# How two streamed weight panels inside the state-space scan reach TensorE: plain float32, or split in high and low parts

## The reference, cut to what matters

```
(z_s, xbc, dt_s, qkv, z_d, b_d, a_d, gate_s, gate_d) = split(u @ w_in[l])
y_s = ssd_chunked(xs, dt, a, Bm, Cm) + xs * d_skip            # the scan, two chunks of 128 tokens
yg  = y_s * silu(z_s);  yg = yg * rsqrt(mean(yg*yg per group)) * norm_w
merged = sigmoid(gate_s) * (y_s @ ssm_w_branch) + sigmoid(gate_d) * (y_d @ dn_w_branch)
h = h + merged @ w_out
```

## Time and profile before

| what | value |
|---|---|
| median of three executions | 2237.24 us |
| the profiled execution's own time | 2238.61 us |
| its span, first to last instruction | 2236.7 us |
| TensorE matmul busy | 2130.2 us (95%) |
| VectorE busy | 1332.4 us (60%) |
| ScalarE busy | 1136.3 us (51%) |
| GpSimd busy | 81.5 us (4%) |
| mean granted TensorE clock | 0.985 of full |
| plain matmul records, line 600 | 384 |

### The profile page before, as it was taken

The page is one execution under the profiler, slowest core; times in us unless marked ns, Lnnn a source line. Parts: engine busy times, 40 slices in busy tenths (PEclk is TensorE's granted clock), DMA queues, the critical chain, the costliest instruction groups (busy, mean ns, idle before and its releaser), DMA issues. The chain is left out here.

```text
span 2236.7 us, 40879 instructions
## 1 busy us (share of the span) xinstructions
PE 2130.2 (95%) x15572; PEld 1863.2 (83%) x15572; DVE 1332.4 (60%) x1845; ACT 1136.3 (51%) x1673; POOL 81.5 (4%) x90
## 2 busy tenths in 40 slices
PE   5999889999999999989999999999999998999998
PEld 4787778887888988888998887887997897998887
DVE  3436375556556986566656555555896575756554
ACT  3453644445445556654445445445556664535444
POOL 0000000000000011100000000000002010000000
PEclk9999999999999999989999999999999999999999
DMA  9663245554553544421455554555444431455553
GB/s 395 240 243 114 76 144 186 188 188 173 186 189 137 179 169 132 170 96 58 151 188 184 188 188 169 184 187 186 145 176 146 156 114 41 141 181 187 188 188 122
DMA packets 53319, 373.08 MB, mean 167 GB/s; under 512 B 6305, under 2 KB 6305, under 8 KB 9281
## 3 DMA queue, kind: packets, MB, share of 16 engines
q1 hardware_dynamic: 47664, 342.00, 42.4%
q0 software_dynamic: 5520, 29.23, 3.7%
HBM read 370.10 MB, written 1.11 MB: 166 GB/s over the span
## 5 line engine op out<-in xcount | busy, mean ns | idle before, releaser
L1443 ACT ACTIVATE HI<-ring 128x1024 fp32r<-128x1024 f32 x606 | 625.1, 1054 | 741.2 <-PE banks L548 399.3
L1987 DVE TENSOR_TENSOR LO<-ring,HI 128x1024 fp32r<-128x1024 f32 x318 | 389.1, 1226 | 368.8 <-ACT HI L1443 368.4
L1993 DVE TENSOR_TENSOR LO<-ring,HI 128x2048 fp32r<-128x2048 f32 x137 | 314.3, 2294 | 242.3 <-ACT HI L1443 242.3
L512 PE MATMUL banks<-UH,HI 128*128 128x256 f32 x1392 | 406.5, 292 | 2.7 <-DVE LO L1993 2.7
L513 PE MATMUL banks<-UL,HI 128*128 128x256 f32 x1392 | 395.9, 284 | 0.0
L514 PE MATMUL banks<-UH,LO 128*128 128x256 f32 x1392 | 395.6, 284 | 0.0
L546 PE MATMUL banks<-HI,UH 128*128 128x512 f32 x896 | 350.0, 391 | 7.1 <-DVE LO L1993 4.9
L547 PE MATMUL banks<-LO,UH 128*128 128x512 f32 x896 | 349.4, 390 | 0.0
L548 PE MATMUL banks<-HI,UL 128*128 128x512 f32 x896 | 349.4, 390 | 0.0
L512 PEld LDWEIGHTS banks<-UH,HI 128*128 128x128 f32 x1392 | 268.8, 193 | 19.8 <-issue 19.1
L513 PEld LDWEIGHTS banks<-UL,HI 128*128 128x128 f32 x1392 | 269.2, 193 | 1.4 <-issue 1.2
(11 more groups left out here) (329 smaller groups left out, 3092.7 us busy)
## 6 DMA issues: line engine op xcount, KB each, us to landing
ring<-in_w_stream SPq DMA_DIRECT2D x315, 1024.0 KB, 4.8
ARENA<-in_ada_stream POOLq DMA_DIRECT2D x16, 1024.0 KB, 5.5
ARENA<-in_ada_stream SPq DMA_DIRECT2D x8, 1024.0 KB, 14.8
GRMS<-cum_rows POOLq DMA_DIRECT2D x16, 256.0 KB, 3.6
ARENA<-in_na_bias POOLq DMA_DIRECT2D x2, 1024.0 KB, 13.4
RMS<-cum_rows POOLq DMA_DIRECT2D x8, 256.0 KB, 3.4
RSTD<-cum_rows POOLq DMA_DIRECT2D x8, 256.0 KB, 3.5
ARENA<-in_ropes POOLq DMA_DIRECT2D x1, 1088.0 KB, 19.1
```

What stands on the lines that cost most here:

```text
L512: nc.tensor.matmul(out, lh, rh, start=start, stop=False, **kw)
L1443: nc.scalar.activation(HI[:, q % PARTS, at], ring[:, q % RING, at], ACT.Copy).then_inc(hi_ready, 1)
L1987: nc.vector.tensor_tensor(LO[:, q % PARTS, at], ring[:, q % RING, at], HI[:, q % PARTS, at].bitcast(F32), ALU.subtract).then_inc(lo_ready, 1)
L1993: nc.vector.tensor_tensor(LO[:, q % PARTS, :], ring[:, q % RING, :], HI[:, q % PARTS, :].bitcast(F32), ALU.subtract).then_inc(lo_ready, 2)
```

## The change

The range of plain panels is cut to 20 to 23, and a new constant `EARLY` = 26 takes over where the code meant the first panel after the scan. Panels 24 and 25 are used in split form within the scan. Three things in the code change and one follows without a changed line:

- TensorE calls `wide_half` instead of `plain_half` in steps 12 to 15.
- GpSimd gets two calls of `split`, for panels 24 and 25, behind its last `load_rows` and ahead of the adding of squares.
- The loop after the scan and VectorE's early low part go by `EARLY`, so panel 26 is treated as before.
- In ScalarE's code the test `if j + PARTS not in PLAIN: ahead(LQ_WIDE + j)` now holds for j = 22 and 23. So in its steps 11 and 13 it writes `HI` of panel 24 and 25, ahead of the `conv_in` of those steps, and `conv_in` no longer counts on `hi_ready` for them. The counters that show panels 24 and 25 as finished become the ordinary ones.

```
-PLAIN = range(20, 26)
+PLAIN = range(20, 24)
+EARLY = 26
...
                     load_rows(i)
+                for j in range(PLAIN[-1] + 1, EARLY):
+                    split(Q_LAYERS + LQ_WIDE + j, L_PANELS * l)
...
                     if i in Z_SLOTS:
                         j, e = Z_SLOTS[i]
-                        plain_half(w0 + j, Q_LAYERS + LQ_WIDE + j, rounds, j % 2, e)
+                        wide_half(w0 + j, Q_LAYERS + LQ_WIDE + j, rounds, j % 2, e)
...
-                    if L_CONV + j not in PLAIN:
+                    if L_CONV + j >= EARLY:
                         for e in range(2):
                             wide_half(w0 + L_CONV + j, Q_LAYERS + LQ_WIDE + L_CONV + j, rounds, j % 2, e,
-                                      l + 1 if L_CONV + j == PLAIN[-1] + 1 else None)
+                                      l + 1 if L_CONV + j == EARLY else None)
...
-                q26 = Q_LAYERS + LQ_WIDE + PLAIN[-1] + 1
+                q26 = Q_LAYERS + LQ_WIDE + EARLY
```

## The result

The changed kernel takes 2245.95 us (median of nine executions, 2241.13 to 2246.9); the kernel before, on the same chip, takes 2237.5 (nine, 2234.84 to 2239.43). The ratio is 1.0037, its 95% interval 1.0028 to 1.0045: 8.5 us or 0.37% slower. The profiled execution took 2246.9 us, its span is 8.4 us longer than that of before.

The account below looks back on a forecast made before the run. TensorE's own instructions were taken to bound scan steps 12 to 15. Stall 4.0 + clock 1.4 - matmuls 1.75 = 3.65 us a layer, 7.3 in two, gave a median of 2244.5 us, range 2240.3 to 2249.5.

Parts of the forecast that it names:

- Bound: Scan steps 12 to 15: TensorE's own instructions set the time, busy all 18.0 us, with a beat of 4.73 us.
- Matmuls: TensorE's halves in steps 12 to 14 each get 0.58 us shorter; three count, 1.75 us a layer.
- High parts: ScalarE's 1.99 us a panel before `conv_in` in steps 11 and 13 costs nothing, hidden with 0.6 us to spare.
- Low parts: GpSimd's subtraction for panel 24 waits for panel 23's last matmul; TensorE stands still 4.0 us, ends 3.76 and 5.1.
- 0.5 us is left: VectorE's `scan_out(7)` behind panel 26's subtraction, 902.5, against release by TensorE at about 903: 0.5 us of slack.
- Rival E: VectorE, shut out twice by GpSimd, brings `scan_out(14)`, `scan_out(15)` or panel 26 late: 2 us more a layer, 2250; chance 0.06.
- Clock: TensorE runs at half clock behind the idle stretch before panel 24: 1.4 us a layer, between 0 and 2.9.
- the sum: Per layer 4.0 (stall) + 1.4 (clock) - 1.75 (matmuls) = 3.65 us; two layers 7.3.
- Rival A: The forecast: one stall before panel 24 in each layer and half clock behind it, 2241.7 to 2249.6 us; chance 0.70.
- B: The stall before panel 24 without a fall of the clock: 2.3 us a layer, 2241.7 (2240.4 to 2244); chance 0.13.
- D: The stall happens, but a later wait, on squares or VectorE, takes most back: 2238 to 2239 us; chance 0.06.
- C: Panel 24's `LO` is there in time, the matmuls' gain stands alone: 3.5 to 4.5 us less, 2233.3; chance 0.05.

Follow-up runs that it names:

- early subtraction: The changed kernel, with GpSimd subtracting for panel 24 once its high part is there, on its own semaphore, not waiting for panel 23: 2236.71 us, ratio 0.9992.
- the filled stall: The changed kernel, with 33 unneeded matmuls on TensorE ahead of its wait for panel 24's low part: 2243.31 us, ratio 1.0023.
- the second measurement: The changed kernel measured again without an edit, on the chip of the experiments: 2244.84 us against 2238.31 before the change, ratio 1.0030.
- the swap: VectorE's last `scan_out` put ahead of panel 26's subtraction; here in the changed kernel with 33 unneeded matmuls before TensorE's wait: 2244.01 us, ratio 1.0027.
- the four kernels with an early low part: The changed kernel with GpSimd early; that with VectorE's last `scan_out` first; VectorE subtracting panels 24, 25; or 22 to 25: 2236.71, 2231.31, 2231.44, 2230.35 us.
- the last three swaps: VectorE's last `scan_out` ahead of panel 26's subtraction, in the changed kernel, with 33 added matmuls, and with panels 22 to 25 split: 2246.99, 2244.01, 2230.75 us.
- the next kernel: The kernel with GpSimd's early start for panel 24, plus VectorE's last `scan_out` ahead of panel 26's subtraction: 2231.31 us, ratio 0.9972.

## Why the prediction was right

- **Bound.** As put: TensorE's order sets the time in steps 12 to 15. It lost 9.0 us there in two layers, and the span grew by 8.4.
- **Matmuls.** 0.58 us a half and 1.75 us for three were predicted; the split half panels at full clock take 3.05 and 3.07, and the kernel with both low parts on VectorE shows 1.77 with nothing else in the way. The 0.96 us a half that I derived from the Trainium skill's 4 passes (FP8 and Floating Point Precision, TensorE Precision Notes) is not what the chip shows. But it rested on a price of 0.12 us for every pass, which the page doesn't give. The sixteen records of a plain half last 3.72 us and the first two of them, in a timeline that ends at 887.0, last 0.70:
```profile
886.61 0.70 PE L600 MATMUL banks<-SQ,ring 128*128 128x256 f32 x2
```
So they start (3.72 - 0.70) / 14 = 0.216 us apart, two for each k-step. If each were two passes, a pass would take 0.108 us, an estimate, and four passes would fit the 3.65. The records show no passes, so neither the count nor that price is shown.
- **High parts.** Forecast: nothing, with 0.6 us to spare. 0.69 is left, and `conv_in` is where it was against `scan_out(12)`, within 0.1 us.
- **Low parts.** Start within 1.5 us of 885.8 (886.19, 0.15 after the end of panel 23's last matmul), released by the plain half, stall 4.0 predicted and 3.98 measured, once a layer, none before panel 25 or 26. That the count is the cause and not GpSimd as such is shown from both sides: without the wait the stall is gone (early subtraction), and with VectorE in GpSimd's place it is 1.55, as long as its shorter subtraction makes it. As the rows showed for one pair of instructions, one engine waits for the other's whole instruction: the product took 5.06 us in place of 0.69. GpSimd's record, begun at 886.19 within VectorE's tap of 886.11, is 0.24 us longer than when alone; that the tap held it back is likely, but the record doesn't show it apart. The Trainium skill's rule of the exclusive lock (SBUF — State Buffer, SBUF: two separate sides) says the same.
- **VectorE.** "0.5 us is left" was 0.86: the low part of panel 26 ended at 905.09 for the 902.5 forecast, and TensorE's release came at 905.95 for about 903. Rival E's mechanism is real but hidden: VectorE's queue moves while TensorE stands still anyway. Take the stall away and it costs 1.7 us in the scan of layer 1, or 1.8 at the table load. (By its own terms E is 2244.5 + 2 x 2 = 2248.5, not 2250, and lies inside the range.)
- **Clock.** This term was mis-sized: 1.4 us a layer taken, between 0 and 2.9; 2.3 and 2.1 shown in the scan by the filled stall. I counted one stretch of 3 us at half clock, all of it behind the stall, because the rows are 3 us long. That is the length of the windows and not of the stretches. Windows of 1 us beside the first, in the kernel before, show it (PEclk is the third number from the right):
```profile
318.00:319.00 1.00, 0.00 (x0) 0.00 (x0) 0.42 (x3) 0.77 (x4) 0.00 (x0) 0.96 0.97 410
...
322.00:323.00 1.00, 1.00 (x9) 1.00 (x9) 0.66 (x3) 0.35 (x1) 1.00 (x1) 0.83 0.00 0
```
With 0.1 and 0.3 us in these two it lasted 3.4 us. In layer 0 of the second measurement one such stretch, 3.4 us, follows the stall, a loss of 1.55. In the profiled execution of the kernel after the stretch is 6.8 us, 1.5 within the stall and 5.3 behind it, so that all 24 matmuls are slow, not 14. I had named that ("a second such stretch may follow") and not taken it. So the scan lost 4.61 and 4.37 us, not 3.65: 9.0 for the 7.3 of the sum.
- **Why the time came out close all the same.** The mis-sized clock made the sum 1.7 us too small, which is less than the medians resolve: by them the loss is 8.5 and 6.5 us in two measurements, and 7.3 lies between. That it comes so close is luck in part. The span went up by 8.4, 0.6 less than the scans, because more happens outside them than the 0.6 shows. At the same table loads of ScalarE the kernel after is 5.07 us late behind the scan of layer 0 (902.11 before), 3.23 at 1573.24, 6.28 at 1587.38 and 9.17 behind the scan of layer 1 (1761.91). Between 1575 and 1582 us its clock is 0.55, that of before 1.00; between 1701 and 1705 us it is 1.00, that of before 0.57. These stretches and others differ between executions of one kernel, and here they nearly cancel.
- **Rival A against B.** Both end in a slower kernel. The fall of the clock is shown, so B falls; D falls, since the table load and the wait before the squares (1.00 us, as before) kept their distance; C falls by the stall.
- **Open.** Filling the stall gives back 4.4 us in the two scans. Without the swap VectorE's queue takes 1.9 of them before the table loads, with the swap all of them arrive there. The medians gain 1.5 and 3.0 us, with intervals that overlap each time, so they neither confirm nor deny it. Open is also what gives the four kernels with an early low part (before the last three swaps) some 1 to 5 us more by the median than their scans explain; half-clock stretches outside the scans are a part of it in the profiled executions, and no run here fixes them in place.

## What to carry to other kernels

A panel whose helper work is released by an in-order counter inherits the end of the unit ahead of it, whatever data it needs itself: the first one behind a change of form starts when the old form ends, and its whole duration stands on the path. Give that first one its own semaphore. Look for the engine whose idle gap is long enough and lies early enough, and not for the one with most idle time: GpSimd was 96% idle, needs twice VectorE's time here, and holds VectorE while it works. This second advice rests on the traces (1.75 us in the scan of layer 1); by the medians, 2231.31 and 2231.44 us, GpSimd with an early start does as well. And a short stall of a full TensorE has to be priced with the half clock that may follow it, here 1.6 to 2.4 us on 4; read the length of a half-clock stretch from windows shorter than the stretch.

## What was not expected of the hardware

- After 3.98 us of idle time TensorE's half clock lasted about 6.8 us in one execution and 3.4 in another, with the same work around it; after 1.55 us of idle time there was none. After 1.71 us for VectorE's product there was one of about 3.4 us, and after 1.72 us in the same place of the next kernel none. So in these runs the length of a stall alone does not tell whether the clock falls.
- Useless matmuls in a stall are better than the stall: the same half panel, started as late behind `scan_out(12)`, ended 2.3 us earlier.
- Two GpSimd subtractions in a row held three VectorE taps for 9.85 us in layer 1, while in layer 0 the last tap got in between them (5.65 for the three) and the product behind was held (5.06). The program is the same in both layers.
